# The samples' convolution rows: two contiguous tiles and a store from a tile of its own

## The chip, the cores and the metric

The kernel runs on one core of one Trainium2 chip. The metric is device time in microseconds (us). The core's engines are TensorE (PE, with its weight loads as PEld), VectorE (DVE), ScalarE (ACT), GpSimd (POOL) and SyncE (SP); each takes its own instructions in order and waits on semaphores for the others. All DMA transfers of this kernel are issued by SP.

## What is computed

One decode step of a two-layer trunk runs for a prompt of 512 tokens and for 8 samples of one token each, which share the weights. Layer 0 is a Mamba-2 mixer, layer 1 differential attention, and each is followed by an MLP. The change touches the mixer's causal convolution, and within it the samples alone:

```python
def causal_dwconv(xbc, buf, w, b):
    xpad = jnp.concatenate([buf, xbc], axis=1)     # buf: the last 3 raw rows
    acc = b + xpad[:, 0:length] * w[0]
    for k in range(1, 4):
        acc = acc + xpad[:, k:k + length] * w[k]
    return jax.nn.silu(acc), xpad[:, -3:]          # the new last 3 raw rows
```

A sample brings three old rows (`state_conv`) of 3072 channels and one new row. The outputs are the convolution of the four, and the last three of the four as the new `s_conv`. The prompt's mixer goes on with a chunked state scan: four groups of heads, four chunks of 128 tokens each, and the last state of each group is an output (`p_ssm`).

## The kernel before, in words

All activations lie transposed, channels on the 128 partitions and 520 tokens (512 of the prompt, 8 of the samples) along a partition. Weights come in blocks of 512 KB through a ring of five tiles (`wraw`); ACT and DVE split each block into a high and a low half, and PE multiplies three times per block piece.

The in-projection's 24 column tiles of x, B and C run first. For each, ACT copies the product out of PSUM, among it the samples' 8 columns into `xs4[:, m, :, 3]` (L861). The tile `xs4` (named `xs` in the trace) holds for each partition 24 x 8 x 4 numbers, the four rows of a channel side by side. SP loads the three old rows into `xs4[:, :, :, 0:3]` at the start (L305) and stores `xs4[:, :, :, 1:4]` as `sconv` when ACT has written the last new row (L319). On the chip's side each of these transfers therefore touches 24,576 pieces of three numbers (12 bytes) with a gap of one number behind each. DVE multiplies the four rows by the taps (`sample_conv`, L1175) in three portions, the last of them in the middle of the state scan.

The state scan runs over `g` = 0 to 3. In each group DVE builds the four chunk states in `hst`, one tile for all groups, beginning with a copy out of PSUM (`hst` L1261). SP stores the last of them (`pssm`, L322). So that the tile isn't overwritten while it is read, DVE waits in group g > 0 for the store of the group before:

```python
            if g:
                v.wait_ge(fin_out, 16 * g)
```

SP issues in the order in which its program is written: the store of the prompt's rows (`pconv`, L317), the samples' rows (`sconv`, L319), then the four `pssm` stores, then the loads of the samples' states (`hs`, L327). PE takes the state products of the four chunks ahead of the outputs (L568, L581, L587), and POOL prepares masked operands (`uadtH`, `uadtL`, L400) as far ahead as PE's use of two buffers lets it.

Of the kernel before, what the change touches and what calls it, by code (L numbers as in the profile page):

```python
# [9 lines left out]
ACT = mybir.ActivationFunctionType  # L10
# [3 lines left out]
P = 128  # L14
D = 1024
SEQ = 512
NB = 8
T = SEQ + NB
HALF = T // 2
# [4 lines left out]
NCONV = 24  # L24
# [36 lines left out]
def build(nc, wblk, wdt, x_t, pvec, consts, rope, ssm_in, conv_in, kcache, vcache, ptab,  # L61
# [4 lines left out]
    def at(name, shape, offset, dt=F32):  # L66
        return nc.alloc_sbuf_tensor_at(name, shape, dt, offset=base + offset)

    def sem(name):
        return ctx.enter_context(nc.semaphore(name))  # L70
# [54 lines left out]
    zq = at("zq", [P, 2, T], q0 + 32960)  # L125
    rg = at("rg", [P, NG, T], O_F)
    s0 = O_HID + 49152
    xs4 = at("xs4", [P, NCONV, NB, 4], s0)
    xsm = at("xsm", [P, NCONV, NB, 4], s0 + 3072)
    xsc = at("xsc", [P, NCONV, NB], s0 + 6144)  # L130
    pcv = at("pcv", [P, NCONV, 3], s0 + 6912)
    slr = at("slr", [P, P], s0 + 7200, F32R)
# [45 lines left out]
    G = [GP[i // 2][:, i % 2, :] for i in range(4)]  # L178
# [5 lines left out]
    def pc(name, i=0, n=1):  # L184
# [11 lines left out]
    taken = sem("taken")  # L196
# [9 lines left out]
    cs_in, scv, pss = sem("convstate_in"), sem("sample_conv"), sem("sample_silu")  # L206
# [27 lines left out]
    osq_s, on_mm, on_rd, or_s, ox_s, ohi, olo, cf_s, p1_s = (sem(n) for n in (  # L234
        "o_sq", "o_mm", "o_sum_read", "o_r", "o_normed", "o_hi", "o_lo", "coefs_ready", "map1_scaled"))
    pw_s = sem("page_products")
    st_out, fin_out, kv_out, y_out = sem("conv_rows_out"), sem("final_state_out"), sem("kv_out"), sem("y_out")
    hs_out = [sem("hs_out0"), sem("hs_out1")]
    block = ctx.enter_context(nc.Block())
# [53 lines left out]
    @block.sync  # L293
    def _(sp):
        sp.dma_start(cst[:, 0:2, :], consts[:, 0:2, :]).then_inc(in_one, 16)
        for i in range(4):
            sp.dma_start(hT[:, 2 * i:2 * i + 2, :], x_t[:, 2 * i:2 * i + 2, :]).then_inc(in_x[i], 16)
        sp.dma_start(raw[:, 0, :], wblk[0, :, :]).then_inc(raw_in[0], 16)
        sp.dma_start(pv[:, :], pvec).then_inc(in_pv, 16)
        sp.dma_start(raw[:, 1, :], wblk[1, :, :]).then_inc(raw_in[1], 16)  # L300
        sp.dma_start(cst[:, 2:6, :], consts[:, 2:6, :]).then_inc(in_par, 16)
        sp.dma_start(wdr[:, :, :], wdt).then_inc(in_par, 16)
        for s in range(2, RAW):
            sp.dma_start(raw[:, s, :], wblk[s, :, :]).then_inc(raw_in[s], 16)
        sp.dma_start(xs4[:, :, :, 0:3], conv_in).then_inc(cs_in, 16)  # L305
        sp.dma_start(ptile[:, :], ptab).then_inc(pt_in, 16)

        def stream(a, b):
            for j in range(a, b):
                sp.wait_ge(blk, j - RAW + 1)  # L310
                sp.dma_start(raw[:, j % RAW, :], wblk[j, :, :]).then_inc(raw_in[j % RAW], 16)

        zb, qb_, kb, ob = (BLOCK0[n] + RAW for n in ("z", "q", "k", "o"))
        stream(RAW, zb)

        sp.wait_ge(cv, NCONV)
        sp.dma_start(pconv, pcv[:, :, :]).then_inc(st_out, 16)  # L317
        sp.wait_ge(taken, NCONV)
        sp.dma_start(sconv, xs4[:, :, :, 1:4]).then_inc(st_out, 16)  # L319
        for g in range(NG):  # L320
            sp.wait_ge(h_s, NCH * (g + 1))
            sp.dma_start(pssm[:, g, :], hst[:, NCH - 1, :]).then_inc(fin_out, 16)  # L322

        sp.wait_ge(y_s, NPAIR)
        sp.wait_ge(fin_out, 16 * NG)
        for m in range(2):
            sp.dma_start(hs[:, m, :, :], ssm_in[m, :, :, :]).then_inc(hs_in[m], 16)  # L327
        for m in range(NPAIR):
            sp.wait_ge(hs_new, m + 1)
            sp.dma_start(sssm[m, :, :, :], hs[:, m % 2, :, :]).then_inc(hs_out[m % 2], 16)  # L330
            if m + 2 < NPAIR:
                sp.wait_ge(hs_out[m % 2], 16 * (m // 2 + 1))
                sp.wait_ge(ys_s, m + 1)
                sp.dma_start(hs[:, m % 2, :, :], ssm_in[m + 2, :, :, :]).then_inc(hs_in[m % 2], 16)
            stream(zb + m, zb + m + 1)
        stream(zb + NPAIR, qb_)
        sp.wait_ge(blk, BLOCK0["q"])
        sp.dma_start(ropt[:, :, :], rope).then_inc(rp_in, 16)
        sp.wait_ge(pt_in, 16)

        def page(n, cache, dst, s):
            idx = sp.value_load(ptile[0:1, n:n + 1], min_val=0, max_val=cache.shape[0] - 1)
            sp.dma_start(dst[:, n % 4, :, :].rearrange("p h k -> p (h k)"),
                         cache[bass.ds(idx, 1), :, :].rearrange("o p n -> p (o n)")).then_inc(s[n % 4], 16)


        vb = BLOCK0["v"]
        stream(qb_, kb)
        sp.wait_ge(blk, BLOCK0["k"])
        for n in range(4):  # L350
            page(n, kcache, ktile, kp_in)
        stream(kb, vb)
        for m in range(8 + RAW):
            stream(vb + m, vb + m + 1)
            for n in range(4 + 2 * (m - 4), 6 + 2 * (m - 4)):
                if 4 <= n < NB * PAGES:
                    sp.wait_ge(ss_s, n - 3)
                    page(n, kcache, ktile, kp_in)
        sp.wait_ge(blk, BLOCK0["o"])
        for n in range(NB * PAGES):  # L360
            if n >= 4:
                sp.wait_ge(sv_mm, n // PAGES - 1)
            page(n, vcache, vtile, vp_in)
            if n == 3:
                sp.wait_ge(kq_s, 16)
                sp.dma_start(kt_out, kT[:, :, :]).then_inc(kv_out, 16)
            elif n == 7:
                sp.wait_ge(taken, TILE0["v"] + AH)
                sp.dma_start(vt_out, vT[:, :, :]).then_inc(kv_out, 16)
        stream(ob, NBLK)  # L370
        for m in range(KT):
            sp.wait_ge(h_n, 24 + m + 1)
            sp.dma_start(y_t[:, m, :], hT[:, m, :]).then_inc(y_out, 16)
        sp.wait_ge(st_out, 32)
        sp.wait_ge(fin_out, 16 * NG)
        for i in range(2):
            sp.wait_ge(hs_out[i], 16 * NPAIR // 2)
        sp.wait_ge(kv_out, 32)
        sp.wait_ge(y_out, 16 * KT)
# [431 lines left out]
    def _(sc):  # L811
        own = Own(sc, act)
        A = sc.activation
# [40 lines left out]
        for m in range(NCONV):  # L854
            sc.wait_ge(blk, m + 1)
            if m >= 2:
                sc.wait_ge(cv, m - 1)
            g = 2 * (m % 2)
            A(xr[:, m % 2, 3:3 + HALF], G[g][:, 0:HALF], ACT.Copy).then_inc(xr_in, 1)
            A(xr[:, m % 2, 3 + HALF:3 + SEQ], G[g + 1][:, 0:SEQ - HALF], ACT.Copy).then_inc(xr_in, 1)  # L860
            A(xs4[:, m, :, 3], G[g + 1][:, SEQ - HALF:HALF], ACT.Copy).then_inc(taken, 1)  # L861
            highs(m + 1 + HIS)
            if m:
                silu_tile(m - 1)
            if m == 6:

                sc.wait_ge(dt_u, 1)
                sc.preload_act_table_set(LN_EXP)
                own(A(dtl[:, :], dtu[:, :], ACT.Abs))
                own(A(dtl[:, :], dtl[:, :], ACT.Exp, scale=-1.0))  # L870
                A(dtl[:, :], dtl[:, :], ACT.Ln, bias=misc[0:32, 9:10]).then_inc(dt_l, 1)
            elif m == 12:
                sc.wait_ge(dtx_mm, 1)
                A(dtx[:, :, :].rearrange("p q b -> p (q b)"), W[1][:, 0:P], ACT.Copy).then_inc(dtx_s, 1)
            elif m == 16:
                sc.wait_ge(dex_mm, 1)
                sc.wait_ge(sda_s, 1)
                A(dex[:, 0:2, :].rearrange("p q b -> p (q b)"), W[3][:, 0:2 * P], ACT.Exp)
                A(dex[:, 2, :], dex[:, 2, :], ACT.Exp).then_inc(dex_s, 1)  # L879
# [27 lines left out]
        for m in range(NPAIR):  # L907
            if m % 4 == 0:
                g = m // 4
# [117 lines left out]
        for n in range(16):  # L1027
# [6 lines left out]
            m = n % 8  # L1034
# [81 lines left out]
    def _(v):  # L1116
        own = Own(v, dve)
        TT, STT, TS = v.tensor_tensor, v.scalar_tensor_tensor, v.tensor_scalar
# [52 lines left out]
        def sample_conv(a, b):  # L1171

            v.wait_ge(taken, b)
            for k in range(4):
                own(TT(xsm[:, a:b, :, k], xs4[:, a:b, :, k],  # L1175
                       pc("conv_w", 24 * k + a, b - a).unsqueeze(2).broadcast_to([P, b - a, NB]), ALU.mult))
            own(v.tensor_reduce(xsc[:, a:b, :], xsm[:, a:b, :, :], AXX, ALU.add))
            TT(xsc[:, a:b, :], xsc[:, a:b, :], pc("conv_b", a, b - a).unsqueeze(2).broadcast_to([P, b - a, NB]),
               ALU.add).then_inc(scv, 1)
# [14 lines left out]
        for m in range(NCONV):  # L1194
# [33 lines left out]
            a = cacc[:, m % 2, :]  # L1228
# [15 lines left out]
        for g in range(NG):  # L1244
# [27 lines left out]
                ssd_out(n - 1)  # L1272
            if g == 0:
                sample_conv(17, NCONV)
            if g + 1 < NG:
                x_dt(g + 1, 0)
                x_dt(g + 1, 1)
# [6 lines left out]
        for m in range(NPAIR):  # L1284
            g = m // 4
# [386 lines left out]
```

## Time and profile before

| | |
|---|---|
| three runs | 1785.55, 1787.02, 1788.64 us (median 1787.02) |
| profiled execution | 1786.33 us, its span 1784.6 us |
| PE, PEld busy | 1553.0 us (87%), 1462.0 us (82%) |
| DVE, ACT, POOL busy | 1009.8 us (57%), 656.2 us (37%), 223.7 us (13%) |
| DMA packets | 93,091, of them 54,179 under 512 B |

Start times count from the span's start. The profiled execution lies 1.73 us over its span, and 0.69 us under the median of the three runs. A timeline row has start, length, engine, line, operation, output <- inputs; the bracket behind it tells how long the engine had been idle and what ended that.

### The profile page before, as it was taken

The page shows a single profiled execution, that of the slowest core. Times are in us where ns is not written, and L with a number is a line of the kernel's source. Part 1 is how long each engine was busy: PE and PEld are TensorE (multiplying, and loading weights), DVE is VectorE, ACT ScalarE, POOL GpSimd, SP SyncE. Part 2 cuts the span into 40 slices and gives each one's busy share as a digit, 9 for nine tenths or more (in the row PEclk, how much of TensorE's full clock was granted, in tenths as well). Part 3 has the DMA queues.
Part 4 walks back from the last instruction along what each step waited for, and adds up shares of the span by engine and source line. Part 5 has one row for each costly group of instructions (what it writes and reads, how often), then busy time and mean ns, then how long its engine had stood idle before and what let it go on. Part 6 is the DMA issues. An engine that isn't in the chain of part 4 may idle for free.

```text
span 1784.6 us, 28516 instructions
## 1 busy us (share of the span) xinstructions
PE 1553.0 (87%) x11978; PEld 1462.0 (82%) x11978; DVE 1009.8 (57%) x1339; ACT 656.2 (37%) x1301; POOL 223.7 (13%) x154
## 2 busy tenths in 40 slices
PE   6999706899699699999998799966778899999995
PEld 6999504699599699999998799943357899999994
DVE  6677706989952744224433735998863743234434
ACT  5434201288732433123322432345544442123320
POOL 1001605700300200000000200023311100000002
PEclk9999958999799899999999899978889899999997
DMA  9222990055422122222222131543112122222221
GB/s 164 74 83 95 5 7 9 12 191 222 155 73 94 57 86 95 95 88 91 95 95 95 48 133 57 178 154 119 48 36 83 60 95 93 86 95 95 95 84 48
DMA packets 93091, 160.08 MB, mean 90 GB/s; under 512 B 54179, under 2 KB 54563, under 8 KB 92707
## 3 DMA queue, kind: packets, MB, share of 16 engines
q1 hardware_dynamic: 92962, 158.25, 35.3%
q8 instruction: 95, 1.56, 0.4%
q14 instruction: 34, 0.27, 0.0%
HBM read 142.07 MB, written 16.16 MB: 89 GB/s over the span
## 4 chain that ended last, share of the span: by engine, by line
PE 46%; issue 25%; DVE 21%; another core or an unknown queue 3%; ACT 2%; DMA 2%; POOL 2%; SPq 0%; POOLq 0%; DVEq 0%; ACTq 0%
PE GP L439 14%; PE GP L441 14%; PE GP L440 13%; DVE hT L1339 2%; DVE wL L1126 1%; DVE misc L1487 1%; DVE kq L1440 1%; DVE hs L1292 1%; POOL fT L388 1%; DVE aL L1334 1%; DVE hc L1295 1%; DVE yss L1296 1%; DVE probs L1504 1%; DVE osq L1545 1%
## 5 line engine op out<-in xcount | busy, mean ns | idle before, releaser
L439 PE MATMUL GP<-aH,wH 128*128 128x260 f32 x1920 | 553.3, 288 | 46.5 <-DVE aL L1334 35.5
L441 PE MATMUL GP<-aH,wL 128*128 128x260 f32 x1920 | 548.6, 286 | 0.0
L440 PE MATMUL GP<-aL,wH 128*128 128x260 f32 x1920 | 547.1, 285 | 0.0
L439 PE MATMUL GP<-hidH,wH 128*128 128x260 f32 x1536 | 440.0, 286 | 5.6 <-DVE hidL L1307 5.5
L441 PE MATMUL GP<-hidH,wL 128*128 128x260 f32 x1536 | 435.8, 284 | 0.0
L440 PE MATMUL GP<-hidL,wH 128*128 128x260 f32 x1536 | 434.6, 283 | 0.0
L439 PEld LDWEIGHTS GP<-aH,wH 128*128 128x128 f32 x1920 | 367.6, 191 | 52.2 <-issue 37.5
L1126 DVE TENSOR_TENSOR wL<-wraw,wH 128x1024 fp32r<-128x1024 f32 x216 | 265.2, 1228 | 195.5 <-ACT wH L829 195.0
L440 PEld LDWEIGHTS GP<-aL,wH 128*128 128x128 f32 x1920 | 368.0, 192 | 0.1
L441 PEld LDWEIGHTS GP<-aH,wL 128*128 128x128 f32 x1920 | 367.8, 192 | 0.0
L829 ACT ACTIVATE wH<-wraw 128x1024 fp32r<-128x1024 f32 x216 | 229.1, 1060 | 291.1 <-PE GP L441 290.4
L439 PEld LDWEIGHTS GP<-hidH,wH 128*128 128x128 f32 x1536 | 291.1, 190 | 7.3 <-issue 3.8
L440 PEld LDWEIGHTS GP<-hidL,wH 128*128 128x128 f32 x1536 | 291.0, 189 | 0.3
L441 PEld LDWEIGHTS GP<-hidH,wL 128*128 128x128 f32 x1536 | 290.9, 189 | 0.0
L388 POOL TENSOR_TENSOR fT<-fT,rpost 128x520 f32<-128x520 f32 x32 | 50.8, 1624 | 926.0 <-ACT rpost L819 926.0
L1375 DVE TENSOR_TENSOR rsq<-rel 128x520 f32<-128x520 f32 x64 | 44.8, 700 | 178.4 <-ACT rel L1009 178.4
L1008 ACT ACTIVATE rel<-GP 128x260 f32<-128x260 f32 x64 | 24.8, 388 | 229.3 <-PE GP L441 229.3
L581 PE MATMUL GP<-decay,xdt 128*64 128x128 f32 x256 | 33.9, 283 | 61.2 <-DVE hst L1261 56.7
L581 PEld LDWEIGHTS GP<-decay,xdt 128*64 128x64 f32 x256 | 26.8, 139 | 71.2 <-issue 68.0
L429 POOL TENSOR_TENSOR vtile<-vtile,satt 128x1024 f32<-128x1024 f32 x16 | 32.0, 2005 | 257.8 <-ACT snb L1098 197.2
L891 ACT ACTIVATE decay<-WP 128x512 f32<-128x512 f32 x32 | 19.1, 598 | 122.1 <-PE WP L551 122.1
L400 POOL TENSOR_TENSOR uadtH<-cst,adtH 128x512 fp32r<-128x512 f32 x32 | 40.1, 1252 | 175.7 <-ACT dex L879 113.1
(252 smaller groups left out, 1774.4 us busy)
## 6 DMA issues: line engine op xcount, KB each, us to landing
wraw<-wblk SPq DMA_DIRECT2D x216, 512.0 KB, 3.2
hs<-ssm_in SPq DMA_DIRECT2D x16, 512.0 KB, 3.6
sssm<-hs SPq DMA_DIRECT2D x16, 512.0 KB, 3.4
ktile<-kcache SPq DMA_DIRECT2D x16, 512.0 KB, 3.5
vtile<-vcache SPq DMA_DIRECT2D x16, 512.0 KB, 4.3
hT<-x_t SPq DMA_DIRECT2D x4, 520.0 KB, 5.6
kt_out<-kT SPq DMA_DIRECT2D x1, 2080.0 KB, 10.8
vt_out<-vT SPq DMA_DIRECT2D x1, 2080.0 KB, 9.9
```

The source lines that it names most:

```text
L388: pool.tensor_tensor(fT[:, m, :], fT[:, m, :], rpost[:, :], ALU.mult).then_inc(fr_s, 1)
L400: pool.tensor_tensor(dst[:, k % 2, :].rearrange("p (c l) -> p c l", c=NCH), cst[:, C_UP:C_UP + 1, :].broadcast_to([P, NCH, P]), src[:, :]. ...
L429: pool.tensor_tensor(x, x, satt[:, pg, :].rearrange("p (h b) -> p h b", h=AH)[:, :, b:b + 1] .broadcast_to([P, AH, P]), ALU.mult).then_inc ...
L439: pe.matmul(out, lh, rh, start=first, stop=False)
L440: pe.matmul(out, lh, rl, start=False, stop=False)
L441: return pe.matmul(out, ll, rh, start=False, stop=last)
L581: ins = pe.matmul(G[n % 2][64 * e:64 * e + 64, c * P:(c + 1) * P], xdt[:, c, (2 * q + e) * 64:(2 * q + e) * 64 + 64], dec[:, k % 4, c * P: ...
L829: A(wH[:, j % HIS, :], raw[:, j % RAW, :], ACT.Copy).then_inc(w_hi, 1)
L1008: A(rel[:, m % 2, HV[0]], G[gb][:, 0:HALF], ACT.Relu)
L1126: TT(wL[:, j % RAW, :], raw[:, j % RAW, :], wH[:, j % HIS, :].bitcast(F32), ALU.subtract).then_inc(w_lo, 1)
L1339: STT(hT[:, m, :], fT[:, m, :], pc(gpost, m), hT[:, m, :], ALU.mult, ALU.add).then_inc(h_n, 1)
L1375: TT(rsq[:, m % 2, :], rel[:, m % 2, :], rel[:, m % 2, :], ALU.mult).then_inc(u_sq, 1)
```

## The change

The tile `xs4` becomes two: `cin` with the three old rows, 576 numbers in one piece per partition, and `xnew` with the new row. The load fills `cin`; ACT writes `xnew`; `sample_conv` reads its first three taps' rows from `cin` and the fourth from `xnew`. A third tile, `cout`, in the place of the products `xsm`, takes the rows to be stored: after the last portion of `sample_conv`, in group 0, DVE waits for that portion's end and copies two rows from `cin` and one from `xnew` into it. SP's store of `sconv` reads `cout` and moves behind the first `pssm` store, with a wait for the copies (`convstate_ready`).

```diff
-    xs4 = at("xs4", [P, NCONV, NB, 4], s0)
+    cin = at("cin", [P, NCONV, NB, 3], s0)
+    xnew = at("xnew", [P, NCONV, NB], s0 + 2304)
     xsm = at("xsm", [P, NCONV, NB, 4], s0 + 3072)
+    cout = at("cout", [P, NCONV, NB, 3], s0 + 3072)
...
-        sp.dma_start(xs4[:, :, :, 0:3], conv_in).then_inc(cs_in, 16)
+        sp.dma_start(cin[:, :, :, :], conv_in).then_inc(cs_in, 16)
         sp.dma_start(ptile[:, :], ptab).then_inc(pt_in, 16)
...
         sp.dma_start(pconv, pcv[:, :, :]).then_inc(st_out, 16)
-        sp.wait_ge(taken, NCONV)
-        sp.dma_start(sconv, xs4[:, :, :, 1:4]).then_inc(st_out, 16)
         for g in range(NG):
             sp.wait_ge(h_s, NCH * (g + 1))
             sp.dma_start(pssm[:, g, :], hst[:, NCH - 1, :]).then_inc(fin_out, 16)
+            if g == 0:
+                sp.wait_ge(cs_s, 1)
+                sp.dma_start(sconv, cout[:, :, :, :]).then_inc(st_out, 16)
...
-            A(xs4[:, m, :, 3], G[g + 1][:, SEQ - HALF:HALF], ACT.Copy).then_inc(taken, 1)
+            A(xnew[:, m, :], G[g + 1][:, SEQ - HALF:HALF], ACT.Copy).then_inc(taken, 1)
...
-                own(TT(xsm[:, a:b, :, k], xs4[:, a:b, :, k],
+                own(TT(xsm[:, a:b, :, k], cin[:, a:b, :, k] if k < 3 else xnew[:, a:b, :],
...
             if g == 0:
                 sample_conv(17, NCONV)
+                v.wait_ge(scv, 3)
+                own(v.tensor_copy(cout[:, :, :, 0:2], cin[:, :, :, 1:3]))
+                v.tensor_copy(cout[:, :, :, 2], xnew[:, :, :]).then_inc(cs_s, 1)
```

SP's queue of the kernel before, from the last of the early loads to the loads of the samples' states (line, operation, out<-in, shape of the transfer; `xs_96` is `xs4`):

```order
L305 DMA xs_96<-conv_in 128x192x3
L306 DMA ptile<-ptab 1x16
L311 DMA wraw<-wblk 128x1024 [waits blk_used] x24
L317 DMA pconv<-pcv 128x72 [waits conv_done]
L319 DMA sconv<-xs_96 24576x1x3 [waits taken]
L322 DMA pssm<-hst 128x512 [waits state_ready] x4
L327 DMA hs<-ssm_in 128x1024 [waits final_state_out,y_ready]
```

The same stretch of SP's queue in the changed kernel:

```order
L308 DMA cin<-conv_in 128x576
L309 DMA ptile<-ptab 1x16
L314 DMA wraw<-wblk 128x1024 [waits blk_used] x24
L320 DMA pconv<-pcv 128x72 [waits conv_done]
L323 DMA pssm<-hst 128x512 [waits state_ready]
L326 DMA sconv<-cout 128x576 [waits convstate_ready]
L323 DMA pssm<-hst 128x512 [waits state_ready] x3
L331 DMA hs<-ssm_in 128x1024 [waits final_state_out,y_ready]
```

The load and the store are now 128 rows of 576 numbers, and one `pssm` store stands ahead of `sconv` instead of none.

DVE in the changed kernel, from the last portion of `sample_conv` in group 0 to the first state copy of group 1:

```order
L1179 TENSOR_TENSOR xsm<-cin,pv 128x56 [waits dve_step] x2
L1179 TENSOR_TENSOR xsm<-xnew,pv 128x56 [waits dve_step]
L1181 TENSOR_REDUCE xsc<-xsm 128x56 [waits dve_step]
L1182 TENSOR_TENSOR xsc<-xsc,pv 128x56 [waits dve_step]
L1280 COPY cout<-cin 128x192x2 [waits sample_conv]
L1281 COPY cout<-xnew 128x192 [waits dve_step]
L1189 TENSOR_TENSOR xdt<-WP,dtt 128x512 [waits x_transposed,ydiag_mm]
```

The two copies at L1280 and L1281 are new; the rows around them stand as before.

## Rows read from the trace of the kernel before

**Rows 1.** The page's chain that ended last, shares of the span by engine.
```profile
PE 46%; issue 25%; DVE 21%; another core or an unknown queue 3%; ACT 2%; DMA 2%; POOL 2%; SPq 0%; POOLq 0%; DVEq 0%; ACTq 0%
```

**Rows 2.** Chain of waits, 195 to 225 us: start, length, what.
```profile
218.70 59.30 another core or an unknown queue
```

**Rows 3.** Waits, 180 to 420 us: total us, times, longest.
```profile
DVE hst L1261 <- DMA pssm<-hst: 59.8, 1, 59.8
PE GP L581 <- DVE hst L1261: 56.7, 1, 56.7
```

**Rows 4.** Timeline of SP's queue, 179 to 198 us: start, length, operation.
```profile
180.51 0.63 SPq L319 DMA_DIRECT2D sconv<-xs  x1
197.50 66.20 SPq L322 DMA_DIRECT2D pssm<-hst  x1
```

**Rows 5.** DMA issues by line: KB each, median us from issue to landing.
```profile
pssm<-hst SPq DMA_DIRECT2D x4, 256.0 KB, 2.4
...
xs<-conv_in SPq DMA_DIRECT2D x1, 288.0 KB, 23.6
sconv<-xs SPq DMA_DIRECT2D x1, 288.0 KB, 95.6
```

**Rows 6.** The pssm tile's four transfers: time to landing.
```profile
DMA to landing us min/median/max: 2.3/2.4/80.5
```

**Rows 7.** Timeline of DVE, 203 to 340 us: start, length, operation, idle before.
```profile
210.86 0.22 DVE L1178 TENSOR_TENSOR xsc<-xsc,pv 128x56 f32<-128x56 f32 x1
210.99 1.28 DVE L1185 TENSOR_TENSOR xdt<-WP,dtt 128x512 f32<-128x512 f32 x2
...
278.02 0.69 DVE L1261 COPY hst<-GP 128x512 f32<-128x512 f32 x1 [59.81 <-DMA pssm<-hst]
...
306.85 0.69 DVE L1261 COPY hst<-GP 128x512 f32<-128x512 f32 x1 [0.53 <-PE GP L568]
...
337.87 0.69 DVE L1261 COPY hst<-GP 128x512 f32<-128x512 f32 x1 [0.53 <-PE GP L568]
```

**Rows 8.** Busy time by stretch: stretch, length, engines, granted clock, DMA share, GB/s.
```profile
218.75:278.02 59.27, 3.39 (x10) 1.52 (x8) 0.00 (x0) 0.75 (x2) 5.44 (x6) 0.55 1.59 7
278.02:306.85 28.83, 24.30 (x147) 19.09 (x148) 24.97 (x33) 6.79 (x12) 17.02 (x15) 0.92 0.03 11
306.85:337.87 31.02, 26.63 (x157) 19.69 (x156) 27.98 (x33) 7.55 (x14) 25.34 (x21) 1.00 0.02 9
...
360.50:1784.60 1424.10, 1282.63 (x10032) 1223.13 (x10030) 776.07 (x1007) 545.52 (x1091) 120.37 (x66) 0.94 0.28 98
```

**Rows 9.** Timeline of DVE, 14 to 32 us, the same columns.
```profile
14.49 0.29 DVE L1141 CAST wdh<-wdr 128x256 fp32r<-128x256 f32 x1
...
17.58 3.48 DVE L1150 TENSOR_TENSOR sq<-fT,rpre 128x520 f32<-128x520 f32 x2
...
24.39 0.69 DVE L1150 TENSOR_TENSOR sq<-fT,rpre 128x520 f32<-128x520 f32 x1
...
30.40 0.21 DVE L1166 CAST slr<-cst 128x128 fp32r<-128x128 f32 x1
```

**Rows 10.** Timeline of POOL, 0 to 32 us.
```profile
16.78 7.13 POOL L393 TENSOR_TENSOR sq<-fT,rpre 128x520 f32<-128x520 f32 x4 [16.33 <-ACT rpre L819]
```

**Rows 11.** Timeline of POOL, 203 to 212 us.
```profile
204.99 1.36 POOL L400 TENSOR_TENSOR uadtL<-cst,adtL 128x512 fp32r<-128x512 f32 x1
211.76 1.04 POOL L413 TENSOR_TENSOR xde<-xdt,dex 128x512 f32<-128x512 f32 x1 [5.41 <-DVE xdt L1185]
```

**Rows 12.** Timeline of SP's queue, 5 to 32 us.
```profile
8.42 20.19 SPq L306 DMA_DIRECT2D ptile<-ptab  x1
30.75 0.36 SPq L311 DMA_DIRECT2D wraw<-wblk  x1
```

**Rows 13.** Waits, 0 to 60 us.
```profile
ACT wH L829 <- DMA wraw<-wblk: 0.7, 1, 0.7
```

**Rows 14.** Busy time by stretch, late in the run.
```profile
1400.00:1720.00 320.00, 320.00 (x2675) 319.88 (x2674) 128.52 (x156) 96.47 (x156) 0.00 (x0) 1.00 0.27 93
```

More of the change, by code:

```diff
@@ L236, in build @@
     pw_s = sem("page_products")
+    cs_s = sem("convstate_ready")
     st_out, fin_out, kv_out, y_out = sem("conv_rows_out"), sem("final_state_out"), sem("kv_out"), sem("y_out")
```

## The prediction

> **What bounds the kernel now.** The page's chain of what ended last comes first: most of the span is PE, "issue" and DVE, but 3% of it, some 50 us, is put down to "another core or an unknown queue" [rows 1]. One core runs, so this can only be a transfer. The chain of waits in order of time shows that it is one piece: 59.30 us from 218.70 us on [rows 2]. The table of waits around it names the waiter: DVE's first state copy of group 1 waits 59.8 us for the transfer `pssm<-hst`, and PE, which needs the state, waits 56.7 us for that copy [rows 3]. The other engines stand still too: in this stretch DVE is busy 0.00 us, and PE's granted clock averages 0.55 of full speed, near the lower of its two levels (1.2 of 2.4 GHz), while it has almost nothing to do [rows 8].
>
> Why does a 256 KB store take so long? Its median landing time is 2.4 us [rows 5], but the slowest of the four took 80.5 us [rows 6]. That is the first one: issued at 197.50, landed at 278.0, and the copy starts at 278.02 [rows 4, 7]. Its own issue lasted 66.20 us. Ahead of it in the same queue stands `sconv`, issued at 180.51, which took 95.6 us for 288 KB [rows 4, 5], so it landed at 276.1 and the state store 1.9 us behind it. From one side the cost is the store's small pieces: 24,576 of 12 bytes, where a state store has 128 rows of 2,048 bytes. From the other it is the order of the queue.
>
> **The store, and what goes.** The changed kernel does two things against the same wait: it stores 128 rows of 2,304 bytes, and it issues this store behind the first state store. Either alone frees the first state store. I bound the new store's landing by the state store's 2.4 us (256 KB, rows nearly as long) and the old 95.6 us; I take 2.4 x 288/256 = 2.7 us. The first state store is then to land some 2.4 us after its issue at 197.50, about 200, and DVE asks for it at 218.7. So the whole wait of 59.30 us goes. What is late next at that copy is PE's state product, as in group 2, whose copy waits 0.53 us for PE and no transfer [rows 7].
>
> SP's new wait for DVE's copies holds back only what is queued behind it: the second state store, which can't start before group 1's last chunk anyway. Issued at about 212, the new `sconv` has until group 2's first copy at about 250 less 2.4 us for the state store behind it, so it could take 35 us before DVE waited for it.
>
> **What is given back: 2.19 us.** While DVE stood still, POOL and PE worked ahead for group 1. The stretch from its first copy to group 2's is 28.83 us; the next such stretch, with nothing done ahead, is 31.02 us [rows 8]. DVE runs the same 33 instructions in both, but with 24.97 against 27.98 us busy, and POOL does 15 operations against 21. Group 1 without the wait should look like group 2. The bounds are 0 (all of the work ahead again finds a hole) and twice 2.19 us; I take 2.19, the nearest row.
>
> **What is added: 0.7 us.** DVE gets two copies on 128 partitions, 384 and 192 numbers, inside a run of work without a hole, on the path to the next group. Single-input operations of this kind between SBUF tiles took 0.21 us for 128 numbers and 0.29 for 256 [rows 9], so 0.08 per 128 more: 0.37 and 0.25, together 0.62. The new wait for the portion's last addition costs the overlap that today's next operation has with it: that one starts at 210.99, the addition ends at 210.86 + 0.22 = 211.08 [rows 7], 0.09 us. The sum is 0.71. The lower bound is two of the short rows, 0.42. The upper bound is a copy held up by POOL: the DVE multiplications beside POOL's at 17 us took 3.48 us for two, 1.74 each, against 0.69 for one alone [rows 9, 10]. Two copies of 1.74 make 3.5 us. But POOL has ended its operation at 206.35 there and starts the next at 211.76, and only on DVE's `xdt`, which comes behind the copies [rows 11]. I take 0.7.
>
> The Trainium skill has a rule that speaks against these copies: SBUF — State Buffer, section "SBUF: two separate sides", says that DVE in its two-port modes (which a single-input fp32 copy can use) and GpSimd share a pair of ports under an exclusive lock, and whichever comes second waits for the other's whole instruction. The trace agrees at 17 us (1.74 against 0.69). By that rule the copies here would meet nobody and the sum stays; if POOL did run late, it would be 2.8 us higher, at the upper bound above.
>
> Reading from `cin` and `xnew` instead of `xs4`, and ACT's write to `xnew`, move the same numbers through the same instructions: 0, with the 128x56 addition's 0.22 us as a size beside which no stride shows.
>
> **The load at the start: 0.** The old load landed in 23.6 us [rows 5] and kept SP for 20.19 us in the issue of the small transfer behind it, until 28.61. SP's next issue, a weight block, comes at 30.75 [rows 12], when PE has freed a buffer; it is not late. DVE reads these rows only at group portions far later. The largest gain that I allow is the one wait of ACT for a weight block in the first 60 us, 0.7 us [rows 13]; a loss I exclude, since fewer pieces pass through the same queue.
>
> **The sum.** 1786.33 (the profiled execution, 1784.6 us of span and 1.73 around it) - 59.30 + 2.19 + 0.70 = 1729.9 us. The median of the runs is 0.69 us above the profiled execution, so 1730.6 us.
>
> **Rivals.**
>
> *The small pieces stay.* If the store from `cout` still went out in pieces of 12 bytes, the second state store would sit behind it. Issued at about 211.8, the store would land at 307.4 and the state store at 309.3, while DVE wants it at 218.7 + 0.7 + 31.0 = 250.4: a wait of 58.9 us in group 2 in place of group 1. Group 2 would then have its work done ahead (28.83 for 31.02), so group 3's first copy would come at 338.1 against 337.87 now [rows 7]: 1787.3 us, no change. For it speaks that only the tile's shape was changed, not the transfer's size; against it the state stores, from a tile of the same kind, and the queue's rows, which show 128x576 where 24576x1x3 stood.
>
> *PE's clock takes the time back.* The wait is also 59 us in which PE rests. If PE were granted less later because it no longer rests, the remaining 1424.1 us, now at a mean of 0.94 [rows 8], would stretch. From 0.94 to 0.90 that is 1424.1 x (0.94/0.90 - 1) = 63.3 us, and the kernel would take 1793.9 us, slower. The point from which it decides is 0.905, where the 56.4 us are used up. Against it: from 1400 to 1720 us PE is busy 320.00 of 320 us and still granted 1.00, the higher level [rows 14], and the low values stand beside waits, as 0.55 in this one and 0.92 in the stretch behind it [rows 8]. So rest seems to cost clock, not to earn it.
>
> **How the numbers follow.** The forecast has 95 in 100, the small pieces 3, the clock 2. The forecast's own range: below, no work given back and 0.7 us won at the start, and copies of 0.42 (1787.02 - 59.3 - 0.7 + 0.4 = 1727.4, and 0.9 for the runs' scatter, whose three values lie within 1.6 us of their median): 1726.5. Above, copies of 3.5 us and a little more given back or scattered (1730.6 + 2.8 + 1.6): 1735. The rivals hold 5 in 100 and stay outside. About 0.2%, 3.6 us, is what a measurement of this kernel can tell from no change: faster 0.95, same 0.03, slower 0.02.
>
> **What would show it.** Right: no DVE wait for `pssm` in the state scan; four landings of `pssm` near 2.4 us; `sconv` landing in some 3 us; packets under 512 B down by 49,152 from the two transfers; some 31 us from one group's first copy to the next, three times; the copies' two rows near 0.37 and 0.25 us; the stages behind the scan as long as before. Wrong: a wait for `pssm` in another group, a `sconv` landing of tens of us, a granted clock under 0.94 in the stages behind the scan, or copies that stand behind a POOL operation.

## The result, and the profile after

The changed kernel takes 1725.92 us (median of four runs, 1721.49 to 1729.06) where the kernel before took 1787.83 (1785.55 to 1789.57): a ratio of 0.9653, 95% interval 0.9628 to 0.9678. That is 61.9 us less. The forecast was 1730.6 us, 56.4 less, with a range of 1726.5 to 1735: the way was right, the time 4.7 us too high, and the measured median lies 0.6 us under the range.

The page's chain of what ended last no longer has the unknown queue that held 3% [rows 1]:

```profile
PE 49%; issue 25%; DVE 22%; POOL 2%; ACT 1%; DMA 1%; SPq 0%; POOLq 0%; DVEq 0%; ACTq 0%
```

The waits in the state scan, 180 to 360 us (total, times, longest), have no `pssm` in them any more; the first state copies of the four groups wait for PE's state products alone [rows 3]:

```profile
DVE hst L1265 <- PE GP L572: 3.3, 4, 1.1
DVE hs L1296 <- DMA hs<-ssm_in: 3.0, 1, 3.0
```

SP's queue, 170 to 310 us (start, length, operation), and the landing of the three kinds of transfer (KB each, median us) answer to [rows 4, 5]:

```profile
196.56 0.34 SPq L323 DMA_DIRECT2D pssm<-hst  x1
210.87 0.33 SPq L326 DMA_DIRECT2D sconv<-cout  x1
```

```profile
pssm<-hst SPq DMA_DIRECT2D x4, 256.0 KB, 2.4
...
cin<-conv_in SPq DMA_DIRECT2D x1, 288.0 KB, 10.2
sconv<-cout SPq DMA_DIRECT2D x1, 288.0 KB, 2.1
```

The store lands in 2.1 us where it took 95.6, and each state store in 2.4. SP's issues of the state stores last 0.34 us at most, where the first one took 66.20. Packets under 512 B fell from 54,179 to 5,026:

```profile
DMA packets 44194, 160.08 MB, mean 93 GB/s; under 512 B 5026, under 2 KB 5410, under 8 KB 43810
```

DVE's timeline shows the new copies and the four first state copies [rows 7]:

```profile
186.31 0.69 DVE L1265 COPY hst<-GP 128x512 f32<-128x512 f32 x1 [1.13 <-PE GP L572]
...
209.91 0.22 DVE L1182 TENSOR_TENSOR xsc<-xsc,pv 128x56 f32<-128x56 f32 x1
210.16 0.36 DVE L1280 COPY cout<-cin 128x384 f32<-128x384 f32 x1
210.55 0.29 DVE L1281 COPY cout<-xnew 128x192 f32<-128x192 f32 x1
210.73 1.28 DVE L1189 TENSOR_TENSOR xdt<-WP,dtt 128x512 f32<-128x512 f32 x2
...
220.09 0.69 DVE L1265 COPY hst<-GP 128x512 f32<-128x512 f32 x1 [1.14 <-PE GP L572]
...
250.57 0.69 DVE L1265 COPY hst<-GP 128x512 f32<-128x512 f32 x1 [0.53 <-PE GP L572]
...
281.57 0.69 DVE L1265 COPY hst<-GP 128x512 f32<-128x512 f32 x1 [0.53 <-PE GP L572]
```

The busy time by stretch, with the starts of these first state copies as edges (stretch, length, PE, PEld, DVE, ACT, POOL, granted clock, DMA share, GB/s) [rows 8]:

```profile
186.31:220.09 33.78, 28.13 (x157) 20.40 (x156) 29.75 (x40) 7.58 (x14) 23.73 (x21) 0.95 0.05 17
220.09:250.57 30.48, 26.06 (x157) 19.38 (x156) 26.87 (x33) 7.39 (x13) 22.13 (x19) 1.00 0.03 10
250.57:281.57 31.00, 26.61 (x157) 19.69 (x156) 27.96 (x33) 7.55 (x14) 25.31 (x21) 1.00 0.03 9
...
304.22:1725.10 1420.88, 1284.12 (x10032) 1224.86 (x10030) 772.88 (x1007) 544.79 (x1091) 120.02 (x66) 0.94 0.29 99
```

The first state copy of group 1 comes at 220.09 instead of 278.02, and the loads of the samples' states start at 304.22 instead of 360.50. So the scan and all before it give 56.28 us between the two profiled executions, and the 1424.10 us behind it became 1420.88, another 3.22.

### The profile page after: what moved, and what is told of

The parts are those of the page before. It is cut to its first block, busy times and chain, and to the rows that moved or that the text cites. A ratio compares the mean times of both kernels' runs of the same rounds, so it can differ in the third digit from the quotient of the medians.

```text
span 1725.1 us, 28518 instructions
## 1 busy us (share of the span) xinstructions
PE 1554.3 (90%) x11978; PEld 1463.2 (85%) x11978; DVE 1010.1 (59%) x1341; ACT 655.4 (38%) x1301; POOL 224.7 (13%) x154
## 2 busy tenths in 40 slices
DMA packets 44194, 160.08 MB, mean 93 GB/s; under 512 B 5026, under 2 KB 5410, under 8 KB 43810
## 4 chain that ended last, share of the span: by engine, by line
PE 49%; issue 25%; DVE 22%; POOL 2%; ACT 1%; DMA 1%; SPq 0%; POOLq 0%; DVEq 0%; ACTq 0%
PE GP L443 14%; PE GP L445 14%; PE GP L444 14%; DVE hT L1346 2%; DVE wL L1130 2%; DVE hc L1302 1%; DVE hs L1299 1%; DVE yss L1303 1%; DVE misc L1494 1%; DVE kq L1447 1%; POOL fT L392 1%; DVE misc L1505 1%; PE WP L749 1%; DVE aL L1341 1%; PE GP L729 1%
## 5 line engine op out<-in xcount | busy, mean ns | idle before, releaser
L1236 DVE SCALAR_TENSOR_TENSOR cacc<-xr,pv,cacc 128x512 f32<-128x512 f32 x72 | 54.8, 761 | 2.5
L1067 ACT ACTIVATE probs<-GP,misc 128x128 f32<-128x128 f32 (+3 forms) x64 | 33.1, 521 | 58.9 <-DVE misc L1495 58.9
L1330 DVE TENSOR_TENSOR acc<-acc,sqt 128x520 f32<-128x520 f32 x28 | 19.6, 699 | 58.2 <-ACT sqt L983 57.7
```

Source lines behind the costliest of these rows:

```text
L1067: A(pr[:, n % 4, j, 0:w], G[2 * (n % 2) + j][:, 0:w], ACT.Exp, scale=QK_SCALE, bias=misc[:, 20 + 2 * (n % 2) + j:21 + 2 * (n % 2) + j], ac ...
L1236: ins = STT(a, xr[:, m % 2, k:k + SEQ], pc("conv_w", 24 * k + m), a, ALU.mult, ALU.add)
```

## The experiments

Twelve runs were made: eight further kernels, the changed kernel again, and the kernel before three times more. The times are medians of five or six executions, except for the three of the kernel before, which are single; a profile shows one execution. A stretch from one first state copy to the next is called after its groups, "0 to 1" and so on; "the rest" runs from DVE's first use of the samples' states to the end of the span.

**1. The changed kernel again.**

> The changed kernel again, to see how far the 3.2 us that its profile wins behind the state scan repeat. Theory 1 (chance: the stages behind the scan differ from one execution to the next, whatever the kernel): the median of five comes nearer to the forecast, 1727 to 1731 us, and the scan again ends 56.3 us earlier than before. Theory 2 (the change itself shortens the stages behind the scan): 1723 to 1727 us, with the stretch from the first load of the samples' states to the end some 3 us under the 1424.1 us of before again.

Measured: 1726.64 us (1724.28 to 1729.55), ratio 0.9662 (0.9646 to 0.9677) against eleven runs of before with median 1787.72. The gain repeats at 61 us. Both numbers lie on theory 2's side: the time is under 1727 us, and from the first load of the samples' states (304.93) to the end of the span (1726.1) it is 1421.2 us, 2.9 under the 1424.1 of before. But the before side of that comparison was one profile. Counted as "the rest", this profile has 1417.8 us and the first one 1417.7; three more profiles of the kernel before decide against theory 2 (experiment 8).

**2. The old load with the new store.**

Against the changed kernel:

```diff
-    cin = at("cin", [P, NCONV, NB, 3], s0)
-    xnew = at("xnew", [P, NCONV, NB], s0 + 2304)
+    xs4 = at("xs4", [P, NCONV, NB, 4], s0)
...
-        sp.dma_start(cin[:, :, :, :], conv_in).then_inc(cs_in, 16)
+        sp.dma_start(xs4[:, :, :, 0:3], conv_in).then_inc(cs_in, 16)
...
-                own(v.tensor_copy(cout[:, :, :, 0:2], cin[:, :, :, 1:3]))
-                v.tensor_copy(cout[:, :, :, 2], xnew[:, :, :]).then_inc(cs_s, 1)
+                v.tensor_copy(cout[:, :, :, :], xs4[:, :, :, 1:4]).then_inc(cs_s, 1)
```

> The changed kernel with the old load: the three old rows go into a tile with a gap behind each row, in 24,576 pieces, and DVE makes the stored rows with one copy of 576 numbers in place of two. If the load is worth nothing, as forecast: within 1 us of the changed kernel, the load landing in some 23 us, the copy 0.5 us against 0.65 for the two. Rival: the load's pieces cost something later (the 3 us): some 3 us slower than the changed kernel.

Measured: 1727.59 us (1725.9 to 1731.62), ratio 0.9667 (0.9653 to 0.9682), which overlaps with that of the changed kernel. The load lands in 23.9 us instead of 10.2, and the one copy takes 0.46 us. The load's worth, 0.95 us between the medians, can't be told from none.

**3. The order alone.**

```diff
-        sp.wait_ge(taken, NCONV)
-        sp.dma_start(sconv, xs4[:, :, :, 1:4]).then_inc(st_out, 16)
...
             sp.dma_start(pssm[:, g, :], hst[:, NCH - 1, :]).then_inc(fin_out, 16)
+            if g == 0:
+                sp.wait_ge(taken, NCONV)
+                sp.dma_start(sconv, xs4[:, :, :, 1:4]).then_inc(st_out, 16)
```

> The kernel before with one edit: the store of the samples' rows, still from the gapped tile, stands behind the first state store. The forecast's rival in its pure form: the wait leaves group 1 and comes back in group 2. The store is issued at about 198, right behind the state store, and lands at about 294; the second state store lands 2 us behind it, at 296, where DVE wants it at about 250: a wait of some 45 us, so 1787.0 - 59.3 + 45 + about 0 = 1773 us. Rival: the store's pieces are slow only while something else runs, so that the wait is gone: about 1730 us. For the time behind the scan: theory 1 gives nothing either way, theory 2 (small pieces) leaves it at 1424 us.

Measured: 1773.76 us (1768.32 to 1781.28), ratio 0.9919 (0.9903 to 0.9935). Its waits, 180 to 420 us, and the landing of its `sconv`:

```profile
DVE hst L1262 <- DMA pssm<-hst: 51.5, 1, 51.5
```

```profile
DMA to landing us min/median/max: 100.7/100.7/100.7
```

The wait moved to group 2, as the rival had it, and is 51.5 us long where 45 were expected: the store took 100.7 us, not the 95.6 of the first profile. That was the first sign that this time isn't fixed. The profiled execution took 1781.28 us and was the slowest of the six; their median is within 1 us of the expected 1773.

**4. The contiguous store ahead of the first state store.**

```diff
+        sp.wait_ge(cs_s, 1)
+        sp.dma_start(sconv, cout[:, :, :, :]).then_inc(st_out, 16)
         for g in range(NG):
...
-            if g == 0:
-                sp.wait_ge(cs_s, 1)
-                sp.dma_start(sconv, cout[:, :, :, :]).then_inc(st_out, 16)
```

> The changed kernel with the store of the samples' rows ahead of the first state store again, still from the contiguous tile. SP waits for DVE's copies until about 211, then issues both; the state store lands at about 216, before DVE asks at 218.7 to 220: as fast as the changed kernel within 1 us. Rival: the order carries the gain, and a wait for the state store of group 0 comes back: 1730 to 1745 us.

Measured: 1726.57 us (1723.7 to 1728.71), ratio 0.9659 (0.9643 to 0.9674): the same as the changed kernel. DVE has no wait for `pssm` here either, and the slowest of the four state stores lands in 2.8 us. With experiment 3 this divides the change: the length of the pieces alone gives the whole gain, the order alone 14 of 61 us, and with long pieces the order is worth nothing.

**5. Without DVE's copies.**

```diff
             if g == 0:
-                sp.wait_ge(cs_s, 1)
-                sp.dma_start(sconv, cout[:, :, :, :]).then_inc(st_out, 16)
+                sp.wait_ge(cs_in, 16)
+                sp.dma_start(sconv, cin[:, :, :, :]).then_inc(st_out, 16)
...
-                v.wait_ge(scv, 3)
-                own(v.tensor_copy(cout[:, :, :, 0:2], cin[:, :, :, 1:3]))
-                v.tensor_copy(cout[:, :, :, 2], xnew[:, :, :]).then_inc(cs_s, 1)
```

> The changed kernel without DVE's two copies; the store writes the three old rows as they were loaded, so that the shift of the rows is left out. It prices the copies by themselves. Forecast's term: 0.7 us less than the changed kernel (about 1725.9). Rival, read off the profiles since: the copies shift DVE against POOL, and the stretch from group 0's to group 1's first state copy falls from 33.8 to 31.5 us while the next one grows from 30.5 to 31.0: 1.8 us less (about 1724.8).

Measured: 1725.46 us (1722.56 to 1729.27), ratio 0.9647 (0.9631 to 0.9663). Stretches, the same columns as above:

```profile
187.59:219.09 31.50, 26.53 (x157) 19.39 (x156) 28.04 (x38) 7.39 (x13) 21.21 (x19) 1.00 0.05 19
219.09:250.09 31.00, 26.59 (x157) 19.69 (x156) 27.95 (x32) 7.54 (x14) 25.31 (x21) 1.00 0.03 10
250.09:282.42 32.33, 27.95 (x157) 20.40 (x156) 27.96 (x32) 7.71 (x14) 26.64 (x22) 0.95 0.02 9
```

0 to 1 falls to the expected 31.50 us and 1 to 2 to 31.00, but 2 to 3 is 32.33 at a granted clock of 0.95. So most of what was won came back two stretches later: the three take 94.83 us here and 95.26 in the changed kernel's first profile. The medians differ by 1.2 us, within the scatter.

**6. The copies behind the scan.**

```diff
-            if g == 0:
-                sp.wait_ge(cs_s, 1)
-                sp.dma_start(sconv, cout[:, :, :, :]).then_inc(st_out, 16)
...
             sp.dma_start(hs[:, m, :, :], ssm_in[m, :, :, :]).then_inc(hs_in[m], 16)
+        sp.wait_ge(cs_s, 1)
+        sp.dma_start(sconv, cout[:, :, :, :]).then_inc(st_out, 16)
...
-                v.wait_ge(scv, 3)
-                own(v.tensor_copy(cout[:, :, :, 0:2], cin[:, :, :, 1:3]))
-                v.tensor_copy(cout[:, :, :, 2], xnew[:, :, :]).then_inc(cs_s, 1)
...
         TT(sdx[:, :, :], yT[:, :, SEQ:T], dtx[:, :, :], ALU.mult).then_inc(sdx_s, 1)
+        own(v.tensor_copy(cout[:, :, :, 0:2], cin[:, :, :, 1:3]))
+        v.tensor_copy(cout[:, :, :, 2], xnew[:, :, :]).then_inc(cs_s, 1)
```

> The changed kernel with the two copies moved behind the scan, where DVE waits 3.0 us for the first load of the samples' states, and the store behind that load. If the copies' price is their place on the path: the same gain as without them, 0.7 us by the forecast's term or 1.8 us by the profiles, with 31.5 and 31.0 us between the first state copies. Rival: the store among the loads of the samples' states delays these by its 2 us, and nothing is won.

Measured: 1728.79 us (1721.97 to 1731.15), ratio 0.9657 (0.9637 to 0.9677). 0 to 1 is 31.51 us again, but the next two stretches are slower:

```profile
186.46:217.97 31.51, 26.54 (x157) 19.39 (x156) 28.38 (x39) 7.39 (x13) 21.52 (x19) 1.00 0.03 9
217.97:250.34 32.37, 27.97 (x157) 20.43 (x156) 27.96 (x33) 7.70 (x14) 26.68 (x23) 0.95 0.03 9
250.34:282.62 32.28, 27.86 (x157) 20.56 (x157) 27.44 (x32) 7.39 (x13) 23.72 (x20) 0.94 0.02 9
```

Nothing is won, though not for the rival's reason: the store takes 6.0 us among the loads, and DVE's wait for the first of them is 2.81 us, no longer than before.

**7. The small pieces in a queue of their own.**

```diff
-        sp.wait_ge(taken, NCONV)
-        sp.dma_start(sconv, xs4[:, :, :, 1:4]).then_inc(st_out, 16)
...
         silu_tile(NCONV - 1)
         sc.preload_act_table_set(LN_EXP)
+        sc.wait_ge(taken, NCONV)
+        sc.dma_start(sconv, xs4[:, :, :, 1:4]).then_inc(st_act, 16)
```

> The kernel before with one edit: the store in 24,576 pieces is issued from ACT at the same place, so that it stands in a queue of its own and the state stores are alone in SP's. If the order within one queue makes the wait: the state store lands well before DVE asks for it 21 us later, and the time is that of the changed kernel without copies, 1725 to 1729 us, although the pieces are as many as before. Rival (the pieces hold the transfer engines, whichever queue they stand in): the state store lands tens of us late and part of the wait stays, 1745 us or more. For the time behind the scan: if the small pieces themselves cost the 3 to 4 us there, it comes out at 1729 us or more and that stretch at 1421 us; if not, at 1725 to 1727 and 1418.

Measured: 1749.26 us (1748.45 to 1754.43), ratio 0.9794 (0.9776 to 0.9812). The rival was right. The four state stores' issues on SP (the first numbers are ns: shortest, median, longest) and landing times, and DVE's two waits:

```profile
L321 SPq DMA_DIRECT2D pssm<-hst x4: 332/332/338, 197.5 to 313.6; - x4
...
DMA to landing us min/median/max: 2.4/17.3/35.7
```

```profile
233.26 0.69 DVE L1264 COPY hst<-GP 128x512 f32<-128x512 f32 x1 [15.01 <-DMA pssm<-hst]
...
274.04 0.69 DVE L1264 COPY hst<-GP 128x512 f32<-128x512 f32 x1 [2.19 <-DMA pssm<-hst]
```

In ACT's queue the store still takes 101.6 us, and a state store beside it up to 35.7 us in place of 2.4. SP's issues are no longer held, 0.34 us at most against the 66.20 of [rows 4], but the landing is. The Trainium skill, "DMA: Bandwidth & Descriptors", section "Queues, rings and completion order", says that each transfer engine takes turns between the queues it has work for, a packet at a time. The trace agrees in kind: 35.7 us is less than the 80.5 behind the store in one queue and far more than alone. What the two stores share that makes the second one late is not shown beyond that. The rest is 1417.0 us here, with all the small pieces: no cost of theirs shows behind the scan.

**8. The kernel before, three more profiles.**

> The kernel before once more, for a second profile of it. If the stages behind the scan differ by chance from one execution to the next: the stretch from the first use of the samples' states to the end is anywhere from 1417 to 1424 us, against 1420.7 in the first profile. If they are longer by the change's absence: 1420 us or more again.

> The kernel before, a third profile: how long the store takes from one execution to the next. It was 95.6 and 98.7 us in two profiles, with waits of 59.8 and 62.1 us behind it. If the forecast's missing 4 to 5 us are the wait's size, the store takes 97 us or more here and the wait is 61 us or more. Rival (the stages behind the scan are longer before the change): wait 60 us or less and 1420 us or more from the samples' states to the end.

> The kernel before, a fourth profile, for the same: wait 61 us or more if its size was mis-read from one execution; 60 us or less, with 1420 us or more behind the scan, if the later stages make the difference.

Their waits, 180 to 420 us, in this order; the first profile had 59.8 [rows 3]:

```profile
DVE hst L1261 <- DMA pssm<-hst: 62.1, 1, 62.1
```

```profile
DVE hst L1261 <- DMA pssm<-hst: 65.5, 1, 65.5
```

```profile
DVE hst L1261 <- DMA pssm<-hst: 63.9, 1, 63.9
```

| profile | its time | store landed in | wait | 0 to 1 | 1 to 2 | 2 to 3 | the rest |
|---|---|---|---|---|---|---|---|
| before, first | 1786.33 | 95.6 | 59.8 | 90.77 | 28.83 | 31.02 | 1420.7 |
| before, second | 1784.31 | 98.7 | 62.1 | 93.37 | 28.90 | 31.00 | 1417.4 |
| before, third | 1785.59 | 101.8 | 65.5 | 96.47 | 30.50 | 30.49 | 1413.5 |
| before, fourth | 1785.40 | 99.9 | 63.9 | 94.87 | 31.19 | 30.50 | 1415.2 |
| changed | 1726.89 | 2.1 | none | 33.78 | 30.48 | 31.00 | 1417.7 |
| changed, again | 1727.91 | 2.1 | none | 33.72 | 30.62 | 31.00 | 1417.8 |

No effect of the change on the rest shows: 1413.5 to 1420.7 us before, 1417.7 and 1417.8 after. The wait does differ from one execution to the next, with the store's landing, and the first profile is the lowest of the four. The third and fourth come from one chip, the second from another; the 1.6 us between the third and fourth are no difference of chips.

**9. Half of the store.**

```diff
-        sp.dma_start(sconv, xs4[:, :, :, 1:4]).then_inc(st_out, 16)
+        sp.dma_start(sconv[:, 0:12, :, :], xs4[:, 0:12, :, 1:4]).then_inc(st_out, 16)
```

> The kernel before with half of the store: the rows of the first 12 of the 24 column tiles are stored, the others left out, so 12,288 pieces of 12 bytes. If each piece has its price: landing in 48 to 50 us, the state store behind it at about 231, a wait of DVE of 12 to 13 us in place of 59 to 62, and 1787.8 - 49 = 1739 us. Rival: the queue's rows show this store as 128x96x3 and the full one as 24576x1x3, and the load (128x192x3) took 23.6 us for as many pieces; if the shape of the transfer makes the price, the half lands in some 12 us, there is no wait and the time is 1726 to 1729 us.

Measured: 1742.49 us (1740.33 to 1750.07), ratio 0.9754 (0.9723 to 0.9784). The profiled execution took 1747.84 us. Its `sconv`, and its wait:

```profile
DMA to landing us min/median/max: 56.0/56.0/56.0
```

```profile
DVE hst L1261 <- DMA pssm<-hst: 17.9, 1, 17.9
```

12,288 pieces take 56.0 us, 4.6 ns for each, against 3.9 to 4.1 for each of the 24,576; the price goes with the number of pieces, though not in exact proportion, and the rival's shape of the transfer does not make it. Landing, wait and time all lie over what was expected (48 to 50, 12 to 13 and 1739 us). Why a stored piece costs four times a loaded one is open.

**10. Four planes, no copies.**

```diff
-    xs4 = at("xs4", [P, NCONV, NB, 4], s0)
+    xs4 = at("xs4", [P, 4, NCONV, NB], s0)
...
-        sp.dma_start(xs4[:, :, :, 0:3], conv_in).then_inc(cs_in, 16)
+        sp.dma_start(xs4[:, 0:3, :, :], conv_in).then_inc(cs_in, 16)
...
-        sp.wait_ge(taken, NCONV)
-        sp.dma_start(sconv, xs4[:, :, :, 1:4]).then_inc(st_out, 16)
...
+            if g == 0:
+                sp.wait_ge(taken, NCONV)
+                sp.dma_start(sconv, xs4[:, 1:4, :, :]).then_inc(st_out, 16)
```

> A version without DVE's copies: the four rows lie as four planes of 192 numbers, the load fills planes 0 to 2 and the store reads planes 1 to 3, each one contiguous piece of 2,304 bytes per partition; only the layout of the two arrays in memory differs. The store stands behind the first state store. If the copies cost what the profiles say (31.5 and 31.0 us between the first state copies instead of 33.8 and 30.5): 1.8 us less than the changed kernel, about 1724.8 us; by the forecast's term 0.7 less, 1725.9. Rival: no difference that can be told (1726.6), as with the copies left out, since the executions of one kernel differ by 7 us.

Measured: 1727.13 us (1724.82 to 1731.4), ratio 0.9671 (0.964 to 0.9703). The rival: no difference from the changed kernel that can be told, with one tile and no copy.

```profile
186.07:218.86 32.79, 27.82 (x157) 20.09 (x156) 28.41 (x38) 7.61 (x14) 23.48 (x20) 0.96 0.05 18
218.86:251.25 32.39, 27.96 (x157) 20.59 (x157) 27.50 (x32) 7.38 (x13) 23.86 (x22) 0.94 0.03 9
```

Two of its stretches are again at 0.96 and 0.94 of the clock.

## Why the prediction was wrong in size

*The cause was right.* The store's pieces held the queue, the first state store stood behind them, and DVE, PE and the others stood behind that. Experiment 9 shows the price of the pieces, 3 the queue's part, 4 that long pieces suffice. The rival with the small pieces did not come about; 3 shows what it would have been in its pure form, a wait of 51.5 us in the next group.

*The step that failed* is "So the whole wait of 59.30 us goes": all of it went, but its size was read from one execution, and this one had the shortest wait of the four that are now known. Their mean is (59.8 + 62.1 + 65.5 + 63.9)/4 = 62.8 us, 3.0 more. The same sum worked on each of the four profiles gives 1729.9, 1725.2, 1721.3 and 1722.0 us: one sum, 8.6 us apart by the choice of the profile.

The table sets the terms of the forecast beside the means of the four profiles before and the two after. The wait is there the stretch 0 to 1 less the 31.50 us that it takes with neither wait nor copies (experiment 5).

| term | forecast | from the profiles' means |
|---|---|---|
| profiled execution before | 1786.33 | 1785.41 |
| the wait | -59.30 | -62.37 |
| given back in 1 to 2 | +2.19 | +0.70 |
| added in 0 to 1 | +0.70 | +2.25 |
| all other stretches | 0 | +1.40 |
| from profile to median | +0.69 | -1.48 |
| sum | 1730.6 | 1725.9 |

The wait is the largest of the differences, 3.1 of 4.7 us. The errors in what is given back and what is added cancel. The last row is the second difference in size, 2.2 us: the forecast carried over that the runs of before lie 0.69 us over their profile, but the changed kernel's two profiled executions lie on average 1.48 us over its median. Why is not shown; the changed kernel's four executions scatter by 7.6 us.

The range failed with it: it was laid round the one wait as if that were the same each time. And for the scatter of whole runs it took 1.6 us above but only 0.9 below; with 1.6 below, the measured time would have lain just inside. The time of a run hid the wait's scatter, since in these four profiles the longer waits go with a shorter rest (1420.7 to 1413.5 us), and why they do is open. So is why the store takes 95.6 us once and 101.8 another time.

*The 3.22 us behind the scan* between the two first profiles, which the forecast had at 0, are scatter: four profiles of before have both longer and shorter rests than the two of after. The rival with the clock is out too: the stages behind the scan kept their granted clock of 0.94 [rows 8]. (Its point of decision works out to 0.904, not 0.905.)

*What is added, 0.7 us.* The copies took 0.36 and 0.29 us, where 0.37 and 0.25 were worked out, and DVE's next operation starts 0.82 us after the portion's last addition instead of 0.13: 0.69 more, as forecast. POOL did not meet them. The prediction's rows of DVE beside POOL at 17 us are of a two-input multiplication, not of a copy, and no run here has these copies beside a POOL operation. But 0 to 1 grew by 2.28, not 0.7 (33.78 against 31.50). PE's timeline in the changed kernel shows the rest of it (start, length, operation, and in the bracket the idle time before it):

```profile
211.47 1.26 PE L516 MATMUL WP<-cst,ssdY 128*128 128x128 f32 x8 [0.70 <-DVE xdt L1189]
215.42 0.48 PE L545 MATMUL WP<-uadtH,slr 128*128 128x512 f32 x1 [2.70 <-DVE xdt L1189]
215.73 0.40 PE L546 MATMUL WP<-uadtL,slr 128*128 128x512 f32 x1
215.97 0.41 PE L554 MATMUL WP<-uadtH,hmr 128*128 128x512 f32 x1
216.20 0.61 PE L555 MATMUL WP<-uadtL,hmr 128*128 128x512 f32 x1
216.61 0.63 PE L545 MATMUL WP<-uadtH,slr 128*128 128x512 f32 x1
```

PE pauses 0.70 and 2.70 us for DVE's `xdt`, and then its 512-column products go over from 0.40 to 0.63 us at about 216.3, from the higher to the lower of its two clock levels; the granted clock of the stretch is 0.95. All four profiles with the copies in group 0 (both of the changed kernel, experiments 2 and 4) have this drop in 0 to 1, which takes 33.54 to 33.80 us. Without copies there, experiments 5 and 6 have 31.50 and 31.51 us at 1.00, and experiment 10 has 32.79 at 0.96; but then a drop stands in one or two of the later stretches. From the first state copy of group 0 to DVE's first use of the samples' states it is 121.1 to 121.3 us in the four with copies, and 121.4, 122.7 and 121.5 in experiments 5, 6 and 10. So the drop is not the copies' price: with them it comes in 0 to 1, without them it mostly comes later, and taking them away wins nothing that can be told. What decides in which stretch it falls is open; a pause of 2.17 us stands before products at either level, as the next rows show.

*What is given back, 2.19 us.* It was 30.48 - 28.83 = 1.65 us between the first profiles. But in the third and fourth profile of before 1 to 2 is 30.50 and 31.19 us, at full wait. The work ahead was done there too: PE had 147 products left, as in the first profile, against 157 in a stretch with nothing done ahead [rows 8]. So something was there to be given back; the granted clock was lower, 0.86 and 0.84 against 0.92:

```profile
283.46:313.96 30.50, 26.75 (x147) 20.89 (x148) 25.31 (x32) 6.68 (x12) 19.01 (x17) 0.86 0.03 10
```

```profile
280.88:312.07 31.19, 27.45 (x147) 21.18 (x148) 26.44 (x32) 6.84 (x12) 19.15 (x17) 0.84 0.03 10
```

The same drop made the difference: late in this stretch, behind a pause of 2.17 us, PE's products are at the higher level in the first profile and at the lower one in the third (in the fourth they go over at about 308.2 us):

```profile
303.79 0.47 PE L541 MATMUL WP<-uadtH,slr 128*128 128x512 f32 x1 [2.17 <-DVE xdt L1185]
304.10 0.39 PE L542 MATMUL WP<-uadtL,slr 128*128 128x512 f32 x1
```

```profile
309.36 0.77 PE L541 MATMUL WP<-uadtH,slr 128*128 128x512 f32 x1 [2.17 <-DVE xdt L1185]
309.92 0.63 PE L542 MATMUL WP<-uadtL,slr 128*128 128x512 f32 x1
```

*The load, 0.* It lands in 10.2 us instead of 23.6, and SP's issue behind it takes 0.35 us instead of 20.19, but experiment 2 finds no time in it. The first state copy of group 0 comes at 186.31 us in the first profile and at 186.95 in the repeat, 187.25 before: with four profiles of before between 185.94 and 187.25, this is scatter.

Taken together between the two first profiles: -59.27 (wait) + 2.28 (0 to 1) + 1.65 (1 to 2) - 0.94 (start) = -56.28 at the end of the scan. The forecast's -56.41 for the scan was right to 0.13 us for that one pair, by errors that cancelled, and it is the pair that misled.

## What to carry to other kernels

A store that goes out in small pieces has to be counted in pieces, not in bytes, and what is lost by it is looked for at the next transfer in its queue and at whoever waits for that. A wait whose length is set by a transfer should be read from several executions before it goes into a sum: one profile gives the cause, not the size. Taking an engine's short work off the path is not yet a gain: here a drop of PE's clock in another stretch took it back.

## What the runs showed of the hardware

Stored in pieces of 12 bytes, 288 KB took 95.6 to 101.8 us, about 4 ns for each piece; loaded in as many pieces, the same bytes took 23.3 to 23.9 us, 1 ns each; in pieces of 2,304 bytes the store took 2.1 us. Behind the small store in the same queue, SP's issue of the next transfer lasted 66 to 72 us by itself in the four profiles of before; with the small store in ACT's queue, SP's issues took 0.34 us at most. But the second queue did not get the state stores past the pieces: a 256 KB store of 2.4 us took up to 35.7 us beside them. PE's 512-column products go over from 0.40 to 0.63 us in some executions and not in others behind the same pause of 2.17 us.
